# Cached attention: where two of the four output-projection half tiles stand, and when their weights are fetched

## What is computed

```python
att = attend(q, k, v)                      # for the samples: moba_decode over 32 cached pages
rw, ... = rwkv7_mix(proj[..., ATT_END:], ...)
mix = jnp.concatenate([att, rw], axis=-1) @ w_out          # 2048 x 2048
x1 = layer_norm(DN_ALPHA * x + mix, ln1_g, ln1_b)
```

## Time and profile of the kernel before

| | |
|---|---|
| median of three runs | 3440.74 us |
| the profiled execution, its time | 3439.39 us |
| the profiled execution, its span | 3437.7 us |
| mean granted clock of TensorE | 0.968 |
| TensorE busy | 94% of the span |
| pairs 0 to 3, from the first half tile of pair 0 to the end of the last value step | 1204.3 to 1512.7 us |

### The profile page before, as it was taken

The page is one execution under the profiler, slowest core; times in us unless marked ns, Lnnn a source line. Parts: engine busy times, 40 slices in busy tenths (PEclk is TensorE's granted clock), DMA queues, the critical chain, the costliest instruction groups (busy, mean ns, idle before and its releaser), DMA issues.

```text
span 3437.7 us, 52237 instructions
## 1 busy us (share of the span) xinstructions
PE 3238.3 (94%) x21602; PEld 2605.7 (76%) x21602; DVE 1484.1 (43%) x2489; ACT 537.7 (16%) x1094; POOL 249.0 (7%) x489
## 2 busy tenths in 40 slices
PE   8999989999988878889799999999999999999997
PEld 6888867887754465668588888888888877888886
DVE  1111156655986433323634334334334343444457
ACT  0000044431213422310200000000000001000012
POOL 0000011100000333410000000000000000000000
PEclk9999989999989989889899999999999999999998
DMA  5222100003200466752232233233223322223232
GB/s 156 74 71 66 48 10 10 11 7 108 74 13 1 141 205 213 224 166 62 62 86 79 81 86 83 79 84 86 80 80 86 84 76 79 83 78 91 72 96 75
DMA packets 446358, 289.27 MB, mean 84 GB/s; under 512 B 22937, under 2 KB 434054, under 8 KB 444728
## 3 DMA queue, kind: packets, MB, share of 16 engines
q1 hardware_dynamic: 431940, 246.80, 25.5%
q0 software_dynamic: 14192, 39.21, 3.7%
HBM read 275.46 MB, written 10.49 MB: 83 GB/s over the span
## 4 chain that ended last, share of the span: by engine, by line
PE 85%; DVE 5%; issue 3%; SPq 2%; ACT 2%; DMA 1%; POOL 1%; POOLq 0%; DVEq 0%; ACTq 0%
PE ps L1035 48%; PE ps L566 16%; PE ps L633 7%; PE ps L880 4%; PE ps L1016 3%; PE ps L868 1%; PE ps L843 1%; POOL W L375 1%; SPq L438 1%; PE ps L937 1%; SPq L375 1%; PE ps L846 1%; DMA W<-in_w_in_dram 1%; PE ps L919 0%; DVE BIG L1556 0%
## 5 line engine op out<-in xcount | busy, mean ns | idle before, releaser
L566 PE MATMUL ps<-XT,W 128*128 128x272 f32 (+1 forms) x2496 | 581.9, 396 | 4.1 <-DMA W<-in_w_in_dram 3.3
L566 PEld LDWEIGHTS ps<-XT,W 128*128 128x128 f32 (+1 forms) x2496 | 473.6, 190 | 113.9 <-issue 5.7
L1035 PE MATMUL ps<-XT,W 128*128 128x272 f32 x1408 | 339.0, 394 | 18.4 <-ACT XT L1341 17.8
L1035 PE MATMUL ps<-XT,SUMS 128*128 128x272 f32 x1408 | 337.0, 392 | 0.0
L1035 PEld LDWEIGHTS ps<-XT,W 128*128 128x128 f32 x1408 | 268.6, 191 | 74.8 <-issue 18.2
L1035 PEld LDWEIGHTS ps<-XT,SUMS 128*128 128x128 f32 x1408 | 267.5, 190 | 55.1
L1893 DVE TENSOR_TENSOR U2B<-ps,S1B 128x272 f32<-128x272 f32 x76 | 33.6, 442 | 616.2 <-PE ps L1035 616.2
L1035 PE MATMUL ps<-TD,W 128*128 128x272 f32 x704 | 173.4, 395 | 5.9 <-DVE TD L1807 4.3
L1035 PE MATMUL ps<-BIG,SUMD 128*128 128x272 f32 x704 | 172.0, 393 | 4.2 <-ACT S5B L1369 4.2
L1035 PE MATMUL ps<-BIG,W 128*128 128x272 f32 x704 | 172.1, 393 | 2.4 <-ACT CNB L1347 2.4
L1035 PE MATMUL ps<-T4U,W 128*128 128x272 f32 x704 | 170.3, 395 | 3.0 <-DVE T4U L1807 3.0
(11 more groups left out here) (358 smaller groups left out, 4257.3 us busy)
## 6 DMA issues: line engine op xcount, KB each, us to landing
W<-in_w_up_dram SPq DMA_DIRECT2D x176, 512.0 KB, 4.9
W<-in_w_in_dram SPq DMA_DIRECT2D x38, 1024.0 KB, 5.8
W<-in_w_down_dram SPq DMA_DIRECT2D x64, 384.0 KB, 4.1
W<-in_w_down_dram SPq DMA_DIRECT2D x64, 320.0 KB, 3.8
W<-in_cache_k_dram POOLq DMA_DIRECT2D x128, 128.0 KB, 3.4
W<-in_cache_k_dram SPq DMA_DIRECT2D x128, 128.0 KB, 3.3
W<-in_cache_v_dram POOLq DMA_DIRECT2D x128, 128.0 KB, 3.1
W<-in_cache_v_dram SPq DMA_DIRECT2D x128, 128.0 KB, 2.8
```

The costliest lines, as they stand in the source:

```text
L566: last = nc.tensor.matmul(ps[0:width, 2 * acc + h, 0:HALF], wt[u][:, k, 0:width], XT[:, k, h * HALF:(h + 1) * HALF], start=k == 0, stop=k ...
L1035: last = nc.tensor.matmul(ps[:, bank, 0:HALF], weights[:, k * P:(k + 1) * P], x[:, k], start=start and k == 0, stop=k == kc - 1, skip_grou ...
```

## The change

`FILL` becomes four tiles for each of pairs 0 to 2 and two for pair 3. Of the tiles of a pair, only the first two stay between the key step and the softmax wait on TensorE. The third now stands behind `values(1)`, the fourth behind `values(4)` (`MID`). VectorE's additions follow: the first two tiles before its wait for `pexpd_ev`, the others after the reciprocal. Pair 3 has tiles 12 and 13 before the softmax wait and no others; tiles 14 and 15 stay behind it.

SP issues the weights of two tiles behind round 0 (sixteen pages) of each kind of pages, not before it, and those of 14 and 15 behind round 0 of the last values. The loop over the two rounds is written out, on SP and on POOL, in place of the hardware loop.

```diff
-        FILL = [range(0, 4), range(4, 8), range(8, 11), range(11, 14), range(14, 15), range(15, 16)]
+        FILL = [(0, 1, 2, 3), (4, 5, 6, 7), (8, 9, 10, 11), (12, 13)]
+        MID = {1: 2, 4: 3}
@@ load_pages
-                    if fill:
-                        fill(bp, kind)
-                    with eng.Fori(0, 2) as r:
+                    for r in range(2):
                         for c in range(4):
                             j = 2 * c + b
                             eng.wait_ge(page_free[j], 4 * bp + 2 * kind + r + 1)
                             for g in range(4):
                                 row = eng.value_load(pages[0:1, bass.ds((2 * bp + b) * N_PAGES + c * 4 + g + r * 16, 1)])
                                 eng.dma_start(pg[j][:, g], cache[bass.ds(row, 1)].rearrange("a p n -> (a p) n")).then_inc(page_landed[j], 16)
+                        if fill and r == 0:
+                            fill(bp, kind)
@@ SyncE
-                for i in FILL[bp][2 * kind:2 * kind + 2]:
+                for i in range(4 * bp + 2 * kind, 4 * bp + 2 * kind + 2):
                     if i >= 2:
                         sp.wait_ge(S["half_mm"], i - 1)
                     sp.dma_start(WH[i % 2], wout_v[:, 8:16, i * P:(i + 1) * P]).then_inc(wh_landed[i % 2], 16)
             load_pages(sp, 0, half_weights)
-            for i in (14, 15):
-                sp.wait_ge(S["half_mm"], i - 1)
-                sp.dma_start(WH[i % 2], wout_v[:, 8:16, i * P:(i + 1) * P]).then_inc(wh_landed[i % 2], 16)
@@ TensorE
-                for i in FILL[bp]:
+                for i in FILL[bp][0:2]:
                     half_tile(i)
@@ in the loop over c of the value step
                     if c:
                         values(c - 1)
+                    if c - 1 in MID and bp < 3:
+                        half_tile(FILL[bp][MID[c - 1]])
@@ VectorE
-                for i in FILL[bp][1:]:
-                    half_tile(i)
+                half_tile(FILL[bp][1])
                 dve.wait_ge(S["pexpd_ev"], bp + 1)
                 link(nc.vector.reciprocal(DS[:, 42:43], DS[:, 41:42]))
+                for i in FILL[bp][2:]:
+                    half_tile(i)
```

## The result

The changed kernel took 3410.3 us (median of four runs, 3406.67 to 3414.34), the kernel before 3440.82 beside it: a ratio of 0.9911 with a 95% interval of 0.9894 to 0.9928, 30.5 us less. The forecast was 3417, with a range of 3404 to 3429. The profiled execution took 3414.34 us, 25.0 less than the one of before (3439.39).

What follows compares the result with a forecast made beforehand. Each pair was taken to cost the time from first half tile to values(0) plus 58 us of page issue. Terms of -26.5 (tiles), -4 (loop), +3 (weights), +4 (clock) gave -23.5 us: 3417 us, range 3404 to 3429.

Steps and rivals of the forecast that it cites:

- The first part: From a pair's first half tile to values(0): shrinks by 12.6, 12.3, 5.0 and 5.0 us in pairs 0 to 3.
- The third tile's stop: Tile behind values(1) delays the buffer release by values(2); POOL stands 2.8 us in each of pairs 0 to 2.
- The fourth tile: Tile behind values(4): covered by waits for value pages, costs nothing, 1 us to spare before POOL wants the keys' second buffer.
- What the two tiles cost: Middle tiles behind values(1) and values(4): 2.8 us a pair in pairs 0 to 2, all from the third tile.
- The second part: From values(0) to the next pair's first half tile: some 58 us set by page issue, plus 2.8 us.
- the clock: TensorE at values(0): the new 2.3 us wait could leave a slow stretch, 1 us a pair, +4 us.
- Without a long stop: POOL from round 1 of the values through the next keys: issues 48 pages without a long stop, 47.3 us.
- The written-out loop: Page issue on the queues: one register operation of 0.05 us a page falls away; 8 us at most, taken as -4.
- The keys' weights: Weights between the two rounds of keys slow neighbouring pages: 0 to 3 us a pair, 1 each taken, +3 us.
- the rival in which they run at the low clock: Middle tiles in the value step take 14.8 us each at half the clock; +15 us, 3455 us; 4%.
- more is won: Rival: register operation goes in full (-8), clock stays high, weights are drained; -34.5 us, 3406 us; 20%.
- its own signs: Trace checks: values(0) 18 to 20 us behind first tile, value-page waits some 10 us, POOL's gap 10 to 12, tiles 7.4.

Runs made afterwards that it cites:

- e1_front4: The changed kernel with all four tiles of pairs 0 to 2 in front of the softmax wait again; 3428.97 us, ratio 0.9972 to the kernel before.
- e4_unroll: The kernel before with only the page loop written out, weights still ahead of the pages; 3429.44 us, ratio 0.9971 to the kernel before.
- e7_keys_late: The changed kernel with the weights of a pair's first two tiles behind all 32 key pages; 3413.35 us, ratio 0.9927 to the kernel before.

## Why the prediction was right, point by point

- **The first part.** Forecast -12.6, -12.3, -5.0, -5.0; measured 32.4 - 19.9 = 12.5, 12.3, 4.4 and 5.0. The softmax is what is late next: values(0) comes 18.5 us behind the first tile where nothing disturbs it, and e1_front4, which puts the two tiles back in front, takes this part back.
- **The third tile's stop.** Forecast: POOL stops 2.8 us a pair. The stops were 4.4 in pair 0 and 3.4 in pair 2, longer because the queue reaches them sooner at 0.90 us a page; in pair 1 it was 1.1, behind a stop of another kind (last section).
- **The fourth tile "costs nothing, with 1 us to spare": wrong.** That microsecond came from a rhythm of 0.985 us, while the same sum let the rhythm fall by 0.05. At 0.90 us the queues are at the keys' second buffer first and stop 1.3 us on POOL in each pair.
- **What the two tiles cost: wrong in size.** I put them at 2.8 us a pair, 8.4 in three. The second part grew by 6.2, 8.9 and 6.5 us against e1_front4, 21.6 together. Of this, 12.8 are the stops that POOL's timeline shows behind the tiles (4.4, 1.1, 3.4 and three of 1.3), each on the path once, as I had it. 2.2 are the slow values(0), which I had under the clock. 6.6 stand behind the issue of the last key page, where I had nothing, holding that the key step stays bound by issue. The fuller key step (0.95 and 299 GB/s, for 0.80) and pages landed after 3.6 us in the median, not 3.2, fit this, but e1_front4 has the same 3.6: its cause stays open.
- **"Without a long stop": misread.** The chain of 48 pages had a stop already before, of 3.03 us at the second page of pair 1's round 1 (last section). The prediction's own rows show it: from 1326.99 to 1344.50 it is 17.5 us for fifteen pages' distance, not 14.8. As every kernel has it, the difference that was forecast did not suffer.
- **The written-out loop.** Forecast -4, at most -8, from 0.05 us a page; one page gained 0.085 us and the edit alone -7.7 in the stage and -8.1 in the median. The term was mis-sized by the row that I took: 46 ns is the length of the register operation, not what it takes on the queue, and the operation that stays got shorter too (43 to 37 ns).
- **The keys' weights.** Forecast +3, measured 0 (e1_front4 against e4_unroll, 54.8 and 54.9 us in the mean; in e7_keys_late their wait only moved).
- **The clock.** Forecast +4. After the 2.2 us wait values(0) ran at 1.62, 1.93, 1.94 and 1.08 us and not 1.08: up to a microsecond in three pairs. No middle tile was slow, so the rival in which they run at the low clock did not occur. The Trainium skill, "TensorE: Matmul & The Clock Gate", section "HAM oscillation — how this bites in real kernels", says that waits for transfers between short bursts bring the low clock back each time. The trace agrees: behind waits for pages the clock fell, and the tiles, with no wait before them, took 7.60 us. What I missed is that such waits would now stand in the key step (3.67 us for 1.97 behind the one of 3.70).
- **Missed: the last value step.** The second part of pair 3 fell from 43.9 to 41.0 us, while I had priced the earlier weights of tiles 14 and 15 at nothing. With the loops alone it is 44.9, with the weights back ahead of the pages 43.6. In the kernel before these weights followed the last pages directly, and the wait before values(7) was 3.38 us, 4.95 with the loops alone; it is 1.36 in the changed kernel and 0.84 in e1_front4. That the weights held up the last pages is read from this; no run moved these two alone.

Added up from the profiles, in us:

| term | forecast | measured |
|---|---|---|
| first part, four pairs | -34.9 | -34.2 |
| the middle tiles and the clock | +8.4 and +4 | +21.6 (e1_front4 to changed) |
| the written-out loop | -4 | -7.7 (before to e4_unroll) |
| the keys' weights | +3 | -0.3 (e4_unroll to e1_front4, pairs 0 to 2) |
| the last value step | 0 | -3.9 (the same two, pair 3) |
| sum | -23.5 | -24.5 |

So the first part, the larger term, was right in mechanism and size. That the rest came out right is luck: the tiles were priced 9 us too low, and the loop, the weights and the last step 11 us too dear. Each row compares single profiles, with the scatter said above. The medians gave 30.5; the profiled execution is the slowest of the four, and no trace shows where the others won their 2 to 8 us more. The case "more is won", with 3406 us, had its mechanism in part (the full gain of the loop), and not the quick draining that it needed.

By its own signs the prediction was right on values(0) (18.5 to 19.9 us behind the first tile), on the waits for value pages (7.9 us, all in pair 3) and on the gap of about 3 us eight pages into round 1, in two of three pairs. Three signs went against it. The rhythm was 0.90, below the 0.93 to 0.99 it allowed. The waits at chunk 4 of the keys grew. And POOL's gap before round 1 was 22.0, 14.6, 18.5 and 13.6 us, not 10 to 12. From first tile to first tile it took 80.7, 82.6 and 80.2 us, not 79 to 80.

## What to carry to other kernels

Where a queue must wait for a buffer that an engine frees, look for the work that stands in front of the freeing instruction and move it behind as many releases as the next data still need time to land; the work is free only while the queue has older buffers to fill. Move the transfers that share that queue along with it: here neither move gave without the other what both gave together. Price a register operation by the distance between issues, not by its own length. And when a stage's issues get faster, redo the sum of who waits for whom before calling a stop free: the microsecond that tile four had to spare went with the faster rhythm.

## What the runs showed of the hardware

- GpSimd's page transfers stop for about 3 us at the same two pages in all fourteen profiles, looped or written out: at the second page of round 1 of pair 1's values and at one page of pair 3's keys. In the kernel before and the changed one:

```profile
1330.57 0.55 POOL L375 DMA_DIRECT2D W<-in_cache_v_dram  x1 [3.03 <-issue]
```

```profile
1304.23 0.55 POOL L374 DMA_DIRECT2D W<-in_cache_v_dram  x1 [2.95 <-issue]
```

  The two are 104 pages apart (the second with 2.97 us before, 2.88 after). They don't move with the code around them or with the time. Whether they go by the count of transfers or by the page itself isn't shown, since all kernels ask for the same pages in the same order; what they are was not tried.
- The changed kernel's runs scatter more than one would think from a static program: 3402.47 to 3420.34 us beside one another, with stages of 300.5 to 306.9 us in three profiles and 1904 to 1911 us from L1016 to the end in all profiles. A part of it is TensorE's clock: near 2808 us of the changed kernel, behind a wait of 1.92 us, twelve matmuls take 4.68 us, and the same twelve 2.99 us in the kernel before, behind a wait of 1.60.
